# A decoder layer's opening on one core: first norm from token rows, transfers issued on arrival of others, and the third weight unit in the output buffer

## The chip, the cores and the metric

The kernel runs on one core of one Trainium2 chip. The metric is the device time in microseconds (us) of one execution; the time before is the median of three runs. Engines are named as in the profile: PE is TensorE's matmul (PEld its weight load), DVE is VectorE, ACT is ScalarE, POOL is GpSimd, SP is SyncE, which here only issues transfers.

## What is computed

One layer of a decoder over 256 tokens of width 1024, in float32. Only its opening matters here:

```python
def rms_norm(x, g):
    xf = x.astype(jnp.float32)
    y = xf * lax.rsqrt(jnp.mean(xf * xf, axis=-1, keepdims=True) + RMS_EPS)
    return (y * g.astype(jnp.float32)).astype(x.dtype)

def swiglu(h, w_gate, w_up, w_down):
    return (jax.nn.silu(h @ w_gate) * (h @ w_up)) @ w_down

x = x + 0.5 * swiglu(rms_norm(x, norm_ffn1[l]), ffn1_gate[l], ffn1_up[l], ffn1_down[l])
```

After it come a mixing sub-layer (projections, attention, a recurrent part), a second SwiGLU of the same form (hidden width 2816 in both) and a last norm.

## The kernel before, in words

**Layout.** The residual `x` lies with its features on the partitions, as 8 tiles of 128 features by 256 tokens. Weights come in units of 1024 by 256 (1 MB): unit 0 is the first 256 gate columns, unit 1 the first 256 up columns, unit 2 the next gate columns, and so on; even units use slot 0 and odd ones slot 1 of `raw`, `whi` and `wlo`. Each float32 operand is split into a high and a low part: ACT copies `raw` into `whi` (`hi`, L521, or in quarters `first_hi`, L531), DVE subtracts (`lo`, L875, or `first_lo`, L885), and PE multiplies three pairs (hi by lo, lo by hi, hi by hi). A unit on PE is a chunk of 48 matmuls of 128x128 by 128x256.

**The norm's factor is applied late.** PE multiplies with `x` times the gain only. The factor 1/rms of each token, `rstd` (128 partitions by 256 tokens, the same in every partition), is multiplied in when DVE takes the product out of PSUM: L923 takes the gate product (`gate_taken`) and L942 the up product (`up_taken`). PE's chunk of unit 2 writes the bank that L923 empties, so `chunk(1, 0)` waits for `lo_ready` 3 and for `gate_taken` 1; `chunk(1, 1)`, unit 3, waits for `lo_ready` 4 and `up_taken` 1.

**SP's queue** issues, in this order and with no wait among them: the first constants (128 columns of identity, 128 of 1/1024, two of epsilon), `x` by tokens in two halves of its columns (`x_in0`, `x_in1`), unit 0 in two halves (`w0_in`, then `w_landed[0]`), unit 1, the other constants (848 KB), twelve small rows of vectors, and `rel_bias`. Every later unit n waits for `lo_ready` n-1, which frees its slot: unit 2 for the end of unit 0's low parts, unit 3 for unit 1's.

**PE** runs six warm-up products of the identity with itself as soon as the first constants are there, transposes the gain rows (L1513) and then `x` in four pairs of tiles (L1518) into banks 2, 3, 6 and 7, runs three more warm-up products, and starts `first_chunk(0)`, which goes on pair by pair as `hlo_f` and `w_lo` come. In `first_chunk(1)`, before its third pair, stands `mean_square(0)`: a product of 1/1024 with the summed squares, which gives every partition the mean square of each token. Then come a transpose of the vector rows (L1474) and the bias row's product (L1477), and then chunks without end.

**ACT** loads its table early, then alternates `h_hi` (the gained `x`, high part, L551) and `first_hi` of unit 0. It then squares the four pairs out of PSUM into `x_sq`, which lies in the output buffer (L621), makes the four quarters of unit 1's high part, and takes the root (`rms_root`, L537), for which another table is loaded; the first Silu (L566) has a third. **DVE** alternates `gained_lo` (L894) and `first_lo`, copies `x` from PSUM to SBUF (L1013) after the squares, makes unit 1's low parts, takes the reciprocal of 128x256 (L912) and enters `ffn`. **POOL** adds the four tiles of squares up (L420, L424, L417), clears two pads (L429, L430), and later sends the bias rows and loads the small "lora" matrices, the first of which waits for the bias row's copy (`bias_row_sb`, L967 to L432).

Of the kernel before, what the change touches and what calls it, by code (L numbers as in the profile page):

```python
# [123 lines left out]
first_hi first_lo sq_first sq_one sq_sum last_sq mean_sq rms_ready rstd_ready gained hhi_ready hlo_ready  # L124
# [20 lines left out]
def trunk(nc, A, consts, out):  # L145
    bias_dram = nc.dram_tensor("bias_rows", (H, 16, 384), F32, kind="Internal").ap()
    with ExitStack() as ctx:
# [20 lines left out]
        idle = sb("idle", [P, 2])  # L168

# [22 lines left out]
        with ExitStack() as sc:  # L192
# [10 lines left out]
            x_sq = out_tok[:].rearrange("p a d -> p (a d)").rearrange("p (q m t) -> p q m t", q=4, m=2)  # L203
# [121 lines left out]
        def _(sp):  # L325
# [12 lines left out]
            for f, base, down in FFN:  # L338
                if f == 0:
                    sp.dma_start(raw[0][:, 0:4], gate_w[0][:, 0:4, 0:W]).then_inc(sg["w0_in"], 16)  # L340
                    sp.dma_start(raw[0][:, 4:KD], gate_w[0][:, 4:KD, 0:W]).then_inc(w_landed[0], 16)
                else:
                    load(base, base // 2, 0, gate_w[f][:, :, 0:W])
                load(base + 1, base // 2, 1, up_w[f][:, :, 0:W])
                if f == 0:
# [53 lines left out]
        def _(pool):  # L399
            def squares(q, signal, first, step, pairs=4):  # L400

                for c in range(pairs):
                    pool.wait_ge(signal, first + c * step)
                    pair = x[:, 2 * c:2 * c + 2]
                    if c == 0:
                        pool.wait_ge(sg["mean_sq"], q)
                        nc.gpsimd.tensor_tensor(sqsum[:], pair, pair, ALU.mult).then_inc(sg["sq_sum"], 1)  # L407
                    else:
                        pool.wait_ge(sg["sq_sum"], 5 * q - 1 + c)
# [3 lines left out]
                halves_sum(5 * q - 1 + pairs)  # L413
# [5 lines left out]
            pool.wait_ge(sg["sq_first"], 2)  # L419
            nc.gpsimd.tensor_tensor(sqsum[:], x_sq[:, 0], x_sq[:, 1], ALU.add).then_inc(sg["sq_sum"], 1)  # L420
            for q in range(2, 4):
                pool.wait_ge(sg["sq_first"], q + 1)
                pool.wait_ge(sg["sq_sum"], q - 1)
                nc.gpsimd.tensor_tensor(sqsum[:], sqsum[:], x_sq[:, q], ALU.add).then_inc(sg["sq_sum"], 1)  # L424
# [90 lines left out]
        def _(act):  # L515
# [10 lines left out]
            def first_hi(n, i):  # L526

                if i % 2 == 0:
                    act.wait_ge(sg["w0_in"] if n + i == 0 else w_landed[n], 16)
# [4 lines left out]
            def rms_root(q, cols=slice(0, T)):  # L534

                act.wait_ge(sg["mean_sq"], q + 1)
# [22 lines left out]
            def ffn(f, base, down):  # L559
# [28 lines left out]
                body(0, nexts(0))  # L588
# [24 lines left out]
            act.wait_ge(sg["x_ffn_even"], 1)  # L613
            nc.scalar.activation(idle[:, 0:1], idle[:, 0:1], ACT.Identity)
# [1411 lines left out]
```

## Time and profile before

| what | before |
|---|---|
| median of 3 runs | 653.97 us (652.64 to 654.25) |
| the profiled execution, its own time | 653.73 us |
| its span | 651.9 us |
| PE busy, DVE busy, ACT busy, POOL busy | 635.1, 424.9, 295.8, 95.9 us |
| mean granted TensorE clock | 0.996 |

The span is what the trace covers; 1.83 us of the profiled execution's own time lie around it. A row of the trace names line, engine, operation, output from input. A matmul's row shows its whole passage through the array, which overlaps the next one, so matmuls of 0.28 us follow each other in less than that.

### The profile page before, as it was taken

The numbers are of one execution on the slowest core, as the hardware profiler recorded it, in microseconds if no ns is written. First come the engines' busy times: TensorE is split into PE (matmuls) and PEld (weight loads), VectorE is DVE, ScalarE is ACT, GpSimd is POOL, SyncE is SP. The second block draws the span as 40 slices with busy tenths as digits, with TensorE's granted clock in tenths as the row PEclk, the third lists the DMA queues.
The fourth block names the chain that finished last, engine by engine and source line by source line (L and its number), as shares of the span: only waits on it lengthen the run. The fifth ranks groups of instructions, "written<-read, shape, count | busy, mean of one in ns | idle before, by whom it ended". The sixth has DMA issues, their size and how long they took to land.

```text
span 651.9 us, 15471 instructions
## 1 busy us (share of the span) xinstructions
PE 635.1 (97%) x6726; PEld 620.3 (95%) x6726; DVE 424.9 (65%) x487; ACT 295.8 (45%) x337; POOL 95.9 (15%) x95
## 2 busy tenths in 40 slices
PE   7899999999999999999998999999999999999996
PEld 7799999999999999999987889999999999999996
DVE  4866787665556369968993337877766666665662
ACT  5544454443334174425654544545533444443331
POOL 0325800000112100020004423006000000000120
PEclk9999999999999999999999999999999999999998
DMA  7686555655555335593242222356555566546541
GB/s 258 196 254 208 174 167 185 190 177 178 178 177 193 102 130 182 185 201 113 98 131 67 68 95 73 125 169 193 174 166 180 188 193 192 174 154 197 167 148 64
DMA packets 100607, 105.37 MB, mean 162 GB/s; under 512 B 2196, under 2 KB 98684, under 8 KB 100564
## 3 DMA queue, kind: packets, MB, share of 16 engines
q1 hardware_dynamic: 99348, 101.45, 49.3%
q0 software_dynamic: 1056, 3.02, 2.1%
q8 instruction: 34, 0.56, 0.4%
q10 hardware_dynamic: 160, 0.27, 0.1%
q14 instruction: 9, 0.07, 0.0%
HBM read 103.48 MB, written 1.25 MB: 161 GB/s over the span
## 4 chain that ended last, share of the span: by engine, by line
PE 90%; DVE 5%; ACT 1%; DMA 1%; issue 1%; SPq 0%; DVEq 0%; ACTq 0%
PE two L1404 26%; PE two L1406 25%; PE two L1405 25%; PE two L1400 11%; DVE w_lo L875 2%; DMA w_raw<-in_ffn_gate 1%; DVE hlo_f L894 1%; PE two L1660 1%; PE two L1662 1%; PE two L1661 1%; DVE w_lo L885 0%; PE two L1803 0%; DVE x L1013 0%; ACT KK L763 0%; DVE rstd L912 0%
## 5 line engine op out<-in xcount | busy, mean ns | idle before, releaser
L521 ACT ACTIVATE w_hi<-w_raw 128x2048 fp32r<-128x2048 f32 (+1 forms) x88 | 166.0, 1887 | 264.7 <-PE two L1406 233.8
L875 DVE TENSOR_TENSOR w_lo<-w_raw,w_hi 128x2048 fp32r<-128x2048 f32 (+1 forms) x88 | 203.9, 2317 | 88.5 <-ACT w_hi L521 88.1
L1404 PE MATMUL two<-hlo_f,w_hi 128*128 128x256 f32 x656 | 185.9, 283 | 2.2 <-DVE w_lo L875 2.2
L1406 PE MATMUL two<-hhi_f,w_hi 128*128 128x256 f32 x656 | 184.9, 282 | 0.0
L1405 PE MATMUL two<-hhi_f,w_lo 128*128 128x256 f32 x656 | 184.8, 282 | 0.0
L1404 PEld LDWEIGHTS two<-hlo_f,w_hi 128*128 128x128 f32 x656 | 123.0, 188 | 3.3 <-DVE w_lo L875 3.3
L1405 PEld LDWEIGHTS two<-hhi_f,w_lo 128*128 128x128 f32 x656 | 124.0, 189 | 0.0
L1406 PEld LDWEIGHTS two<-hhi_f,w_hi 128*128 128x128 f32 x656 | 123.9, 189 | 0.0
L1404 PE MATMUL two<-hid_lo_t,w_hi 128*128 128x256 f32 x352 | 99.9, 284 | 0.0
L1406 PE MATMUL two<-hid_hi_t,w_hi 128*128 128x256 f32 x352 | 99.3, 282 | 0.0
L1405 PE MATMUL two<-hid_hi_t,w_lo 128*128 128x256 f32 x352 | 99.3, 282 | 0.0
L1404 PE MATMUL two<-hlo_m,w_hi 128*128 128x256 f32 x288 | 83.7, 290 | 0.3 <-DVE w_lo L875 0.3
L1405 PE MATMUL two<-hhi_m,w_lo 128*128 128x256 f32 x288 | 80.5, 279 | 0.0
L1406 PE MATMUL two<-hhi_m,w_hi 128*128 128x256 f32 x288 | 80.4, 279 | 0.0
L1405 PEld LDWEIGHTS two<-hid_hi_t,w_lo 128*128 128x128 f32 x352 | 66.5, 189 | 0.0
L1404 PEld LDWEIGHTS two<-hid_lo_t,w_hi 128*128 128x128 f32 x352 | 66.2, 188 | 0.2
L1406 PEld LDWEIGHTS two<-hid_hi_t,w_hi 128*128 128x128 f32 x352 | 66.4, 189 | 0.0
L1404 PEld LDWEIGHTS two<-hlo_m,w_hi 128*128 128x128 f32 x288 | 54.2, 188 | 3.8 <-issue 2.3
L1406 PEld LDWEIGHTS two<-hhi_m,w_hi 128*128 128x128 f32 x288 | 54.3, 188 | 0.1
L1405 PEld LDWEIGHTS two<-hhi_m,w_lo 128*128 128x128 f32 x288 | 54.3, 189 | 0.0
L407 POOL TENSOR_TENSOR sqsum<-x 128x512 f32<-128x512 f32 x3 | 3.1, 1040 | 249.1 <-DVE x L991 220.5
L942 DVE TENSOR_TENSOR prod<-two,rstd 128x512 f32<-128x512 f32 x22 | 15.2, 692 | 26.0 <-PE two L1406 26.0
(327 smaller groups left out, 966.2 us busy)
## 6 DMA issues: line engine op xcount, KB each, us to landing
w_raw<-in_ffn_up SPq DMA_DIRECT2D x22, 1024.0 KB, 5.4
w_raw<-in_ffn_gate SPq DMA_DIRECT2D x21, 1024.0 KB, 5.3
w_raw<-in_w_in SPq DMA_DIRECT2D x20, 1024.0 KB, 5.1
w_raw<-in_ffn_down SPq DMA_DIRECT2D x16, 896.0 KB, 4.8
w_raw<-in_ffn_down SPq DMA_DIRECT2D x8, 1024.0 KB, 5.2
w_raw<-in_w_out SPq DMA_DIRECT2D x4, 1024.0 KB, 5.9
w_raw<-in_proj_a SPq DMA_DIRECT2D x4, 512.0 KB, 3.5
w_raw<-in_proj_b SPq DMA_DIRECT2D x4, 512.0 KB, 4.4
```

The source lines that it names most:

```text
L407: nc.gpsimd.tensor_tensor(sqsum[:], pair, pair, ALU.mult).then_inc(sg["sq_sum"], 1)
L521: nc.scalar.activation(whi[slot][:, 0:kts], raw[slot][:, 0:kts], ACT.Copy).then_inc(sg["hi_ready"], 1)
L875: nc.vector.tensor_tensor(wlo[slot][:, 0:kts], raw[slot][:, 0:kts], whi[slot][:, 0:kts].bitcast(F32), ALU.subtract).then_inc(sg["lo_ready" ...
L894: last = nc.vector.scalar_tensor_tensor(out=hl[:, 2 * j + m], in0=src, scalar=v(GAINS[q], 2 * j + m), in1=hh[:, 2 * j + m].bitcast(F32), o ...
L942: nc.vector.tensor_tensor(prod[:], bank[1][:].rearrange("p (m t) -> p m t", m=2), rstd2, ALU.mult).then_inc(sg["up_taken"], 1)
L1400: return mm(dst, lhsT, rhs, start=start, stop=True, skip_group_check=True)
L1404: mm(dst, whi[slot][:, k_, cols], xl, start=start, stop=False)
L1405: mm(dst, wlo[slot][:, k_, cols], xh, start=False, stop=False)
L1406: return mm(dst, whi[slot][:, k_, cols], xh, start=False, stop=stop)
L1660: mm(dst, hlo_m[:, k_, ts], whi[c % 2][:, k_], start=k_ == 0, stop=False)
L1661: mm(dst, hhi_m[:, k_, ts], wlo[c % 2][:, k_], start=False, stop=False)
L1662: last = mm(dst, hhi_m[:, k_, ts], whi[c % 2][:, k_], start=False, stop=k_ == KD - 1)
```

## The change

SP: the second half of unit 0 is issued when the first half of `x` has landed, unit 1 when the second half has, and unit 2 when the first half of unit 0 has landed. Unit 2 goes into the output buffer (`raw2`), so it needs no free slot. The other constants, the vector rows and `rel_bias` follow, and then unit 3, which waits for `lo_ready` 2 as before.

The first norm: ACT squares `x_tok` (tokens on the partitions, 128 by 512, four times) with an accumulated sum per token, DVE adds the two halves' sums, ACT takes the root of a 128x2 tile, DVE its reciprocal, and DVE multiplies the identity by each token's factor and by 1024 (two tiles of 128x128). PE multiplies 1/1024 with these, which puts every token's factor into all partitions, before the fourth pair of `first_chunk(1)`. ACT copies the result to `rstd`. POOL takes no part; its adds are gone. Unit 2's high and low parts are made in halves of 128x1024 straight after the root and after the two diagonal tiles. The table of the root is the one loaded at the start, and a Silu of one column loads the Silu table after the copy.

Order: unit 1's quarters come before the squares, each followed by one square on ACT and by one copy of `x` on DVE. The transpose of the vector rows and the bias row's product go behind unit 2's chunk on PE, and DVE's `bias_sb` goes behind body 1. POOL's clearing of pads waits for the first chunk. PE's warm-up products use a tile of ones that DVE writes, so they wait for no transfer: seven, the transpose of the gains, three, the transposes of `x`, four.

```diff
@@ SP
-                    sp.dma_start(raw[0][:, 0:4], gate_w[0][:, 0:4, 0:W]).then_inc(sg["w0_in"], 16)
-                    sp.dma_start(raw[0][:, 4:KD], gate_w[0][:, 4:KD, 0:W]).then_inc(w_landed[0], 16)
...
+                    sp.dma_start(raw[0][:, 0:4], gate_w[0][:, 0:4, 0:W]).then_inc(w_landed[0], 16)
+                    sp.wait_ge(sg["x_in0"], 16)
+                    sp.dma_start(raw[0][:, 4:KD], gate_w[0][:, 4:KD, 0:W]).then_inc(sg["w0_in"], 16)
+                    sp.wait_ge(sg["x_in1"], 16)
+                    load(1, None, 1, up_w[0][:, :, 0:W])
+
+                    sp.wait_ge(w_landed[0], 16)
+                    sp.dma_start(raw2, gate_w[0][:, :, W:2 * W]).then_inc(w_landed[0], 16)
                     sp.dma_start(cst[:, C_FIRST:C_ALL], consts[:, C_FIRST:C_ALL]).then_inc(sg["const_in"], 16)
                     for name in list(VECS)[1:]:
                         vector_rows(sp, name, sg["vec_in"])
                     sp.dma_start(rel[:], A["rel_bias"]).then_inc(sg["vec_in"], 16)
+                    load(3, None, 1, up_w[0][:, :, W:2 * W])
...
-                with sp.Fori(1, NG) as i:
+                with sp.Fori(1 if f else 2, NG) as i:
@@ POOL
-            pool.wait_ge(sg["sq_first"], 2)
-            nc.gpsimd.tensor_tensor(sqsum[:], x_sq[:, 0], x_sq[:, 1], ALU.add).then_inc(sg["sq_sum"], 1)
...
-            halves_sum(3)
-
...
-            pool.wait_ge(sg["sq_sum"], 4)
+            pool.wait_ge(sg["multiplied"], 1)
@@ ACT
-                body(0, nexts(0))
+                body(0, nexts(0) if f else [lambda: None, nexts(0)[1]])
...
-            nc.scalar.activation(idle[:, 0:1], idle[:, 0:1], ACT.Identity)
+            act.wait_ge(sg["x_ffn_odd"], 1)
+            nc.scalar.activation(idle[:, 0:1], idle[:, 0:1], ACT.Sqrt)
             act.wait_ge(sg["gain1_ready"], 1)
             for j in range(4):
                 h_hi(0, j, hhi_f)
                 first_hi(0, j)
             for j in range(4):
-                act.wait_ge(sg["hlo_ready"], j + 1)
-                nc.scalar.activation(x_sq[:, j], bank[X_BANKS[j]][:].rearrange("p (c t) -> p c t", c=2),
-                                     ACT.Square).then_inc(sg["sq_first"], 1)
-            for j in range(4):
                 first_hi(1, j)
-            rms_root(0)
+                act.wait_ge(sg[f"x_in{j // 2}"], 16)
+                nc.scalar.activation(h_f[:, 2 * j:2 * j + 2].rearrange("p m t -> p (m t)"),
+                                     x_tok[:, j % 2, j // 2 * (D // 2):(j // 2 + 1) * (D // 2)], ACT.Square,
+                                     accum_out=tok[:, j:j + 1]).then_inc(sg["first_norm"], 1)
+            act.wait_ge(sg["first_norm"], 5)
+            nc.scalar.activation(tok[:, 6:8], tok[:, 4:6], ACT.Sqrt, bias=cst[:, C_EPS:C_EPS + 1],
+                                 scale=1.0 / D).then_inc(sg["rms_ready"], 1)
+
+            act.wait_ge(w_landed[0], 32)
+            act.wait_ge(sg["multiplied"], 1)
+            nc.scalar.activation(whi[0][:, 0:4], raw2[:, 0:4], ACT.Copy).then_inc(sg["first_hi"], 1)
+            nc.scalar.activation(whi[0][:, 4:KD], raw2[:, 4:KD], ACT.Copy).then_inc(sg["hi_ready"], 1)
+            act.wait_ge(sg["first_norm"], 8)
+            nc.scalar.activation(rstd[:, 0:T], bank[4][:, 0:T], ACT.Copy).then_inc(sg["first_norm"], 1)
+            nc.scalar.activation(idle[:, 0:1], idle[:, 0:1], ACT.Silu)
             ffn(0, N_FFN1, N_DOWN1)
@@ DVE
             for j in range(4):
-                dve.wait_ge(sg["sq_first"], j + 1)
+                first_lo(1, j)
                 nc.vector.tensor_copy(x[:, 2 * j:2 * j + 2], bank[X_BANKS[j]][:].rearrange("p (c t) -> p c t", c=2))\
                     .then_inc(sg["x_loaded"], 1)
-            for j in range(4):
-                first_lo(1, j)
-            inverse_rms(0)
+            dve.wait_ge(sg["first_norm"], 4)
+            nc.vector.tensor_tensor(tok[:, 4:6], tok[:, 0:2], tok[:, 2:4], ALU.add).then_inc(sg["first_norm"], 1)
+            dve.wait_ge(sg["rms_ready"], 1)
+            nc.vector.reciprocal(tok[:, 6:8], tok[:, 6:8]).then_inc(sg["rstd_ready"], 1)
+            dve.wait_ge(sg["rstd_ready"], 1)
+            for j in range(2):
+                nc.vector.tensor_scalar(prod[:, 0, j * P:(j + 1) * P], ident, tok[:, 6 + j:7 + j], float(D),
+                                        ALU.mult, ALU.mult).then_inc(sg["first_norm"], 1)
+            dve.wait_ge(sg["first_hi"], 7)
+            nc.vector.tensor_tensor(wlo[0][:, 0:4], raw2[:, 0:4], whi[0][:, 0:4].bitcast(F32), ALU.subtract)\
+                .then_inc(sg["first_lo"], 1)
+            dve.wait_ge(sg["hi_ready"], 3)
+            nc.vector.tensor_tensor(wlo[0][:, 4:KD], raw2[:, 4:KD], whi[0][:, 4:KD].bitcast(F32), ALU.subtract)\
+                .then_inc(sg["lo_ready"], 1)
+            dve.wait_ge(sg["first_norm"], 9)
@@ PE
-                    if n == 1 and pair == 2:
-                        mean_square(0)
+                    if n == 1 and pair == 3:
+                        pe.wait_ge(sg["first_norm"], 7)
+                        for j in range(2):
+                            last = part(bank[4][:, j * P:(j + 1) * P], mat("mean_d"), prod[:, 0, j * P:(j + 1) * P], j == 0)
+                        last.then_inc(sg["first_norm"], 1)
...
                     first_chunk(1)
+                    chunk(1, 0)
...
                         .then_inc(sg["bias_row"], 1)
+                    chunk(1, 1)
...
+            pe.wait_ge(sg["x_ffn_even"], 1)
+            warm(7)
             pe.wait_ge(sg["first_in"], 16)
-            for i in range(6):
-                part(bank[4][:, 0:P], ident, ident, True)
             pe.wait_ge(sg["gain1_in"], 16)
             nc.tensor.transpose(bank[5][:, 0:KD], vec_rows[0:KD], ident[0:KD, 0:KD]).then_inc(sg["gain1_T"], 1)
+            warm(3)
...
-            for i in range(3):
-                part(bank[4][:, 0:P], ident, ident, True)
+            warm(4)
```

## Rows read from the trace of the kernel before

**Rows 1.** The page: busy time by engine, and the chain's shares by engine.

```profile
PE 635.1 (97%) x6726; PEld 620.3 (95%) x6726; DVE 424.9 (65%) x487; ACT 295.8 (45%) x337; POOL 95.9 (15%) x95
...
PE 90%; DVE 5%; ACT 1%; DMA 1%; issue 1%; SPq 0%; DVEq 0%; ACTq 0%
```

**Rows 2.** The chain that ended last, opening: start, length in us, what.

```profile
2.17 7.20 DMA w_raw<-in_ffn_gate
...
14.43 0.60 DVE w_lo L885
15.03 2.40 DVE x L1013 x4
17.43 0.78 DVE w_lo L885
...
22.68 1.76 DVE rstd L912
24.47 0.69 DVE silu L923
25.16 2.21 DVE w_lo L875
```

**Rows 3.** Timeline of PE: start, us, row, idle before it and what ended it.

```profile
18.34 0.36 PE L1400 MATMUL two<-hlo_f,w_hi 128*128 128x256 f32 x1 [1.39 <-DVE w_lo L885]
...
24.85 0.25 PE L1474 MATMUL two<-cst,vec_rows 96*128 96x96 f32 x1
25.03 0.81 PE L1477 MATMUL two<-cst,rel 32*8 32x384 f32 x2
27.41 0.39 PE L1404 MATMUL two<-hlo_f,w_hi 128*128 128x256 f32 x1 [1.57 <-DVE w_lo L875]
```

**Rows 4.** Stretch table, all engines: stretch, its length, busy time and count by engine.

```profile
27.40:33.40 6.00, 5.99 (x50) 5.99 (x51) 4.60 (x5) 2.09 (x3) 0.80 (x1) 1.00 0.74 203
```

**Rows 5.** Waits of PE from 34 to 640 us: total, times, longest.

```profile
PE two L1404 <- DVE w_lo L875: 1.3, 3, 0.6
```

**Rows 6.** Timeline of DVE, unit 1's low parts.

```profile
17.34 4.29 DVE L885 TENSOR_TENSOR w_lo<-w_raw,w_hi 128x512 fp32r<-128x512 f32 x4
```

**Rows 7.** Groups by form over the whole span: busy us, mean ns.

```profile
L728 ACT ACTIVATE w_hi<-w_raw 128x1024 fp32r<-128x1024 f32 x8 | 8.2, 1051 | 0.0
...
L537 ACT ACTIVATE rstd<-two,cst 128x2 f32<-128x2 f32 x1 | 0.3, 262 | 1.8 <-PE two L1400 1.8
...
L632 ACT ACTIVATION_READ_ACCUMULATOR lg<-lg,stat 128x1 f32 x16 | 3.0, 186 | 0.0
...
L1348 DVE TENSOR_TENSOR w_lo<-w_raw,w_hi 128x1024 fp32r<-128x1024 f32 x4 | 4.9, 1224 | 0.0
...
L1096 DVE TENSOR_SCALAR lg<-lg,stat 128x128 f32<-128x128 f32 x8 | 2.3, 282 | 0.0
...
L1088 DVE TENSOR_SCALAR stat<-stat 128x2 f32<-128x2 f32 x8 | 1.4, 169 | 0.3
```

**Rows 8.** Timeline of ACT, opening.

```profile
15.53 2.25 ACT L531 ACTIVATE w_hi<-w_raw 128x512 fp32r<-128x512 f32 x4
...
24.47 1.28 ACT L566 ACT_TABLE_LOAD   x1
```

**Rows 9.** Timeline of SP's queue, opening.

```profile
3.81 4.10 SPq L346 DMA_DIRECT2D cst<-in_consts  x1
...
12.22 0.32 SPq L349 DMA_DIRECT2D rel<-in_rel_bias  x1
```

**Rows 10.** Issue to landing: both `x` halves; then units 0 (halves) and 1.

```profile
DMA to landing us min/median/max: 3.6/4.9/6.2
...
DMA to landing us min/median/max: 7.2/8.2/10.6
```

**Rows 11.** Issue to landing of the seven whole units issued between 20 and 60 us.

```profile
DMA to landing us min/median/max: 5.3/5.4/5.9
```

**Rows 12.** Stretch table as in rows 4; the last two columns are DMA share and GB/s.

```profile
0.00:5.00 5.00, 2.03 (x9) 2.03 (x10) 0.09 (x2) 1.49 (x2) 0.20 (x4) 1.00 0.58 183
5.00:10.00 5.00, 5.00 (x28) 4.36 (x26) 1.04 (x3) 1.45 (x4) 0.00 (x0) 1.00 1.05 357
```

More of the change, by code:

```diff
@@ L168, in trunk @@
         idle = sb("idle", [P, 2])
+        tok = sb("tok", [P, 8])
         def mat(name):
@@ L349, in _ @@
                     sp.dma_start(rel[:], A["rel_bias"]).then_inc(sg["vec_in"], 16)
-                with sp.Fori(1, NG) as i:
+                    load(3, None, 1, up_w[0][:, :, W:2 * W])
+                else:
+                    load(base, base // 2, 0, gate_w[f][:, :, 0:W])
+                    load(base + 1, base // 2, 1, up_w[f][:, :, 0:W])
+                with sp.Fori(1 if f else 2, NG) as i:
                     load(2 * i + base, None, 0, gate_w[f][:, :, bass.ts(i, W)])
@@ L528, in first_hi @@
                 if i % 2 == 0:
-                    act.wait_ge(sg["w0_in"] if n + i == 0 else w_landed[n], 16)
+                    act.wait_ge(sg["w0_in"] if n == 0 and i == 2 else w_landed[n], 16)
                 ks_ = slice(2 * i, 2 * i + 2)
@@ L962, in nexts @@
                     return [lambda s=s: lo(2 * i + (base + 2 + s), s) for s in range(2)]
-                body(0, nexts(0))
-                if f == 0:
-                    dve.wait_ge(sg["bias_row"], 1)
-                    nc.vector.tensor_tensor(bias_sb[:], bank[6][0:H, 0:384], cst[0:H, C_NEG:C_NEG + 384],
-                                            ALU.add).then_inc(sg["bias_row_sb"], 1)
+                body(0, nexts(0) if f else [lambda: None, nexts(0)[1]])
                 if f == 0:
@@ L971, in ffn @@
                         body(i, nexts(i))
+                        if i == 1:
+                            dve.wait_ge(sg["bias_row"], 1)
+                            nc.vector.tensor_tensor(bias_sb[:], bank[6][0:H, 0:384], cst[0:H, C_NEG:C_NEG + 384],
+                                                    ALU.add).then_inc(sg["bias_row_sb"], 1)
                 with dve.Fori(1 if f else 9, NG - 1) as i:
@@ L999, in ffn @@
                         gained_lo(1, j)
-            nc.vector.memset(idle[:, 0:1], 0.0).then_inc(sg["x_ffn_even"], 1)
-            nc.vector.memset(idle[:, 1:2], 0.0).then_inc(sg["x_ffn_odd"], 1)
+            nc.vector.memset(silu[:, 0, 0:P], 1.0).then_inc(sg["x_ffn_even"], 1)
+            nc.vector.memset(idle[:], 0.0).then_inc(sg["x_ffn_odd"], 1)
             dve.wait_ge(sg["gain1_T"], 1)
@@ L1484, in ffn @@
                     chunk(0, 1)
-                with pe.Fori(1, NG) as i:
+                with pe.Fori(1 if f else 2, NG) as i:
                     chunk(i, 0)
@@ L1506, in ffn, with warm @@
                         last.then_inc(sg["multiplied"], 1)
+            def warm(count):
+                for i in range(count):
+                    part(bank[4][:, 0:P], silu[:, 0, 0:P], silu[:, 0, 0:P], True)
+            pe.wait_ge(sg["x_ffn_even"], 1)
+            warm(7)
             pe.wait_ge(sg["first_in"], 16)
-            for i in range(6):
-                part(bank[4][:, 0:P], ident, ident, True)
             pe.wait_ge(sg["gain1_in"], 16)
             nc.tensor.transpose(bank[5][:, 0:KD], vec_rows[0:KD], ident[0:KD, 0:KD]).then_inc(sg["gain1_T"], 1)
+            warm(3)
             for q in range(4):
```

26 lines of the change are left out of this document (9 added, 17 removed).

## The prediction

> **What bounds the kernel now.** I read the page first: PE is busy 97% of the span and carries 90% of the chain that ended last [rows 1]. Everything behind the opening is PE at full pace: a stretch of 6.00 us holds 50 matmuls [rows 4], so one takes 0.12 us and a chunk of 48 takes 5.76 us, and from 34 to 640 us PE waits for low parts 1.3 us in all [rows 5]. The change can therefore earn only what PE loses before it runs without gaps, and each microsecond by which that point moves is one off the end.
>
> Next the chain in order of time [rows 2]. To 15.03 us it is DVE, fed by the first half of unit 0 landing at 2.17 + 7.20 = 9.37 us; then four copies of x, unit 1's low parts, the reciprocal, the gate product, unit 2's low part. PE's timeline shows what that costs [rows 3]: first_chunk(0) is over at 18.34 - 1.39 = 16.95 us, PE is idle 1.39 us, first_chunk(1) lasts to 24.85 us with small gaps, and after the two small products PE is idle 1.57 us to 27.41. Unit 2's chunk starts there, so unit 3's starts at 27.41 + 5.76 = 33.17 us. That is the point I move.
>
> **The change, part by part.** *What starts everything.* DVE is free of its first phase at 15.03 us [rows 2]. The waits of DVE in that phase hang on unit 0's first half, whose place in SP's queue is unchanged. Whether holding later transfers back makes it land sooner no row shows. Two bounds. Nothing: it stays at 9.37. Most: 183 GB/s over 5 us and 357 GB/s behind that [rows 12] are about 0.92 MB by 5 us and 1.95 MB by 7.9 us, when x's second half has landed (issue near 1.7 plus 6.2 [rows 10]); 1.18 MB would have been enough for it, so 0.77 MB of later transfers, 2.1 us, went first. Unit 0's first half has 1.70 MB up to its end, reached at 7.2 us; x's first half landed near 1.2 + 3.6 = 4.8 us [rows 10], 0.5 us after the 0.66 MB up to its end had moved at these rates; with so short a lag unit 0's half would land at 7.7, 1.7 us sooner (estimates from the rows named). I take nothing, because the landings from x's second half to unit 1 all come about 2 us behind their bytes, as they would if some of the 16 engines were simply behind on all they hold: holding back what is queued behind does not speed those up. The 1.7 us stay in the range. The Trainium skill speaks against this part too (DMA: Bandwidth & Descriptors, section "Queues, rings and completion order"): each engine consumes the descriptors of its ring in order. By that rule a transfer behind gives way already, and the gain is zero; by the byte count above the sum would end 1.7 us earlier.
>
> *Unit 1 before the squares.* Unit 1 lands at 3.23 + 10.6 = 13.8 us before [rows 10]. Now it is issued at about 7.95; a unit alone takes 5.4 us [rows 11], which is 13.35, and with unit 0's second half still ahead of it I keep 13.8. Its first quarter's high part takes 2.25/4 = 0.56 us [rows 8], so it is ready at 14.4, before DVE is free; it may be 0.6 us late at no cost. DVE then alternates: 4 x (0.60 + 0.60) = 4.80 us, to 19.83 [rows 2]. The low parts took 4.29 us for four [rows 6], against 2.4 at 0.60 each, while POOL was adding; POOL is idle now, so I take 0.60. ACT does 0.56, as much for a square of the same size, and up to 0.19 for reading the accumulator [rows 7, 8]: 4 x 1.3 = 5.2 us, to 19.0, hidden behind DVE. PE gets a quarter every 1.2 us and needs 1.44 for it, so the idle 1.39 us [rows 3] go and first_chunk(1) runs from 16.95 to 22.7 and, with the spread product (at most 0.5 us, since all that first_chunk(1) holds beyond its 48 matmuls now, gaps too, is 24.85 - 18.34 - 5.76 = 0.75 [rows 3]), to 23.2.
>
> *The norm.* From 19.83: add 0.17, root 0.26, with hand-offs about 0.05: 20.3 [rows 7]. On DVE reciprocal 0.17 and two diagonal tiles of 0.28: 21.1. PE reaches the fourth pair at 16.95 + 3 x 1.44 = 21.3, so it hardly waits. Gone are POOL's adds, the 128x256 reciprocal of 1.76 us [rows 2] and one table load of 1.28 us from the path.
>
> *Unit 2.* It lies in the output buffer by about 16 us (issued near 9.5 behind unit 1) and is wanted at 20.3. ACT: half a unit is 1.05 us, ready at 21.35 and 22.35. DVE: 1.22 us per half [rows 7], from 21.35 to 22.57, then to 23.7 (rows of one engine overlap by 0.08). Only then comes the gate product, 0.69 us [rows 2]: 24.4. Unit 2's chunk waits for it, since it writes that bank. This is the new last wait: PE is done at 23.2 and idles 1.2 us. The copy to rstd (about 22.3 to 22.8) and the Silu table (1.28 us, to 24.1 [rows 8]) lie beside it.
>
> *The two small products* stood in PE's gap; now they stand on its path: from 24.85 to 25.84 us they are busy [rows 3], less about 0.3 by which a matmul's passage overlaps the next, 0.7 us. bias_sb on DVE and POOL's bias and lora transfers move back by some 9 us; these cost nothing as long as the lora halves, whose last issue waits for chunk 6 either way, keep their place.
>
> *The start on PE.* Earlier warm-up moves the transposes by a few tenths, but unit 0's landing at 9.37 sets what follows: nothing.
>
> **Sum.** Unit 2's chunk starts at 24.4, ends at 30.15, small products 30.85: unit 3's chunk starts there instead of at 33.17, 2.3 us sooner. Unit 3 must then be ready: issued when unit 1's low parts are done (15.03 + 3 x 1.2 + 0.6 = 19.2), landed at 24.6 [rows 11], its high part (after the first silu, 25.1; two halves of 1.05 [rows 7] make 2.0) and its low part of 2.2 us [rows 2]: 29.3, 1.5 us of room. Against the profiled execution's 653.73 this is 651.4; that execution lies 0.24 below the median 653.97.
>
> **Rivals.** *A: transfers do come sooner.* Unit 0's half at 7.7 and unit 1 by 12.6 shift the whole DVE chain by 1.7 us: 649.7. For it: the 0.77 MB above. Against: the constant lag. Half of it, 650.5, is as good. *B: unit 1 is late,* because three waits stand between issues where none did, or because unit 2 and the constants share the engines with it. Unit 1 and 2 together are 2.1 MB from 9.0 us at 357 GB/s [rows 12]: if they ended together, unit 1 would land at 15 and DVE start at 15.6, 0.6 us later: 652.0; with the constants mixed in too, 17.3 us and 653.0 or more. Against: units issued before it had landed in order. *C: the squares need another table than the root.* Then two loads of 1.28 us enter ACT's chain, the squares end at 20.3, the root at 21.8, 1.5 us later: 652.9. For it: before, the squares ran on a table that the root had to replace. Against: Copy and Identity run on every table there, and Square may. *D, slower: unit 3 behind SP's queue.* The constants took SP 4.10 us to issue and it was done with the small rows at 12.54 us [rows 9], 8.7 us in all; from 9.9 that is 18.6. If it is t instead, unit 3's chunk starts at t + 5.4 + 2.0 + 2.2: it costs from t = 21.2 on, turns slower than before at t = 23.6, and 653.7 + (t - 23.6) is the time: 656.7 at t = 26.6, were the constants to hold SP 12 us with two whole units outstanding. Against: half the backlog of before stands ahead of them.
>
> **How the numbers follow.** A measurement of this kernel can tell about 0.3%, 2 us, from no change: faster means below 652.0. Base case 0.46 (651.4, own spread 0.5 us for the small hand-offs, of which a sixth lies above 652.0), A 0.26, B 0.13, C 0.07, D 0.04, the rest (0.04) beyond A or mixed. Faster: 0.38 + 0.26 + 0.03 from B + 0.02 = 0.69. Slower: 0.03. Same: 0.28. The range goes from A's end less 0.2 to C's, which takes in most of B: 649.5 to 652.9.
>
> **What would show it.** Right: unit 0's half lands at 9.4; DVE rows of 0.6 us alternate with copies to 19.8; PE has no gap between the first two chunks; one gap of 1.2 us before L1404 ended by DVE's gate product; unit 3's chunk near 30.8. Wrong: a landing before 8.5 (A), ACT waiting for unit 1 past 14.5 (B), a table load before the first square (C), ACT waiting for unit 3 past 26.7 (D), or PE losing more than before later on, where I expect nothing to move.

## The result, and the profile after

The changed kernel took 645.97 us (median of 4 runs, 644.80 to 647.58) against 653.67 us for the kernel before on the same chip (652.64 to 654.25): ratio 0.9886, 95% interval 0.9859 to 0.9913. Forecast were 651.4 us and a range of 649.5 to 652.9. The sign was right; the gain is 7.7 us where 2.3 were forecast, and the time lies outside the range.

The page of the kernel after: busy time by engine, and the chain's shares by engine, as in [rows 1].

```profile
PE 630.7 (98%) x6738; PEld 615.9 (96%) x6738; DVE 423.1 (66%) x491; ACT 295.5 (46%) x343; POOL 90.6 (14%) x91
...
PE 88%; DVE 5%; DMA 3%; ACT 2%; issue 0%; SPq 0%; DVEq 0%; ACTq 0%
```

PE has 12 more instructions and is busy 4.4 us less. Nothing that the prediction names makes the same matmuls shorter. To see where the time went I set the starts of the same work side by side (ACT's copies of whole units; most start when PE frees a slot, the one at 424 us when its transfer has landed, in both kernels):

| stretch | before, us | after, us | gain so far | gain in the stretch |
|---|---|---|---|---|
| opening, to ACT's copy of a unit near 45 us | 45.05 | 42.12 | 2.93 | 2.9 |
| to 68 us | 68.09 | 66.10 | 1.99 | -0.9 |
| rest of the first FFN, to 159 us | 158.81 | 155.81 | 3.00 | +1.0 |
| to 328 us | 328.01 | 324.78 | 3.23 | +0.2 |
| small matmuls of the mixing, to 424 us | 423.89 | 417.12 | 6.77 | +3.5 |
| second FFN, to 617 us | 616.59 | 607.97 | 8.62 | +1.9 |
| span | 651.9 | 643.0 | 8.9 | +0.3 |

So only a third of this pair's gain is made in the opening. (The profiled executions lie 653.73 - 644.80 = 8.9 us apart, more than the medians.) Four things have to be explained: the opening, a loss near 60 us, a small steady gain in both FFNs, and a jump in the mixing.

**The opening** is what the prediction drew. The chain that ended last, of the kernel after, in order of time (start, us, what):

```profile
1.66 4.95 DMA x_tok<-in_x
6.63 6.99 DMA w_raw<-in_ffn_up
13.64 0.64 ACT w_hi L531
14.30 0.69 DVE w_lo L895
14.99 0.60 DVE x L1023
...
18.59 0.60 DVE x L1023
...
22.94 0.61 DVE silu L933
23.55 0.14 issue
23.68 0.36 PE two L1426
```

VectorE alternates low parts and copies at 0.60 us each. PE waits 0.95 us inside the first chunk (to 9.59 us), 0.58 us for the diagonal tiles (to 20.46 us), and last and longest for the gate product, as its timeline shows; the two small products stand behind unit 2's chunk:

```profile
23.68 0.36 PE L1426 MATMUL two<-hlo_f,w_hi 128*128 128x256 f32 x1 [1.12 <-DVE silu L933]
...
29.46 0.25 PE L1500 MATMUL two<-cst,vec_rows 96*128 96x96 f32 x1
29.63 0.81 PE L1503 MATMUL two<-cst,rel 32*8 32x384 f32 x2
```

Forecast were 24.4 for the chunk and a gap of 1.2. What the prediction has otherwise is the first line of the chain: unit 1 is now on it, by way of the wait for `x`.

**The loss near 60 us.** Waits of the kernel after from 44 to 66 us (us in total, times, longest):

```profile
ACT w_hi L521 <- DMA w_raw<-in_ffn_gate: 5.4, 1, 5.4
...
PE two L1426 <- DVE w_lo L885: 0.9, 1, 0.9
```

and who shared the engines with that unit, in the timelines of POOL and SP of the same kernel:

```profile
42.04 0.80 POOL L432 DMA_DIRECT2D bias_rows<-bias_sb  x1 [25.39 <-DVE bias_sb L980]
42.83 0.94 POOL L435 DMA_DIRECT2D x_tok<-in_w_lora_a  x1
43.74 0.91 POOL L437 DMA_DIRECT2D x_tok<-in_a_lora_a  x1
44.62 0.78 POOL L441 DMA_DIRECT2D out_tok<-in_g_lora_a  x1
...
46.54 0.37 SPq L331 DMA_DIRECT2D w_raw<-in_ffn_gate  x1
```

POOL waited 25.39 us for the bias row that the change had put behind unit 2's chunk, and then issued four transfers in three microseconds that used to be spread from 32.54 to 45.25 us. The weight unit issued behind them at 46.54 took 9.1 us to land, where [rows 11] have 5.3 to 5.9.

**The jump in the mixing.** By PE's own rows the kernel after is 3.3 us ahead at 338 us of the kernel before, about 5.9 us at 384 and at 415 us, and about 7 us at 443 us. Waits of PE from 338 to 430 us, first the kernel before:

```profile
PE two L1400 <- issue: 2.7, 4, 1.1
```

and after:

```profile
PE two L1422 <- issue: 0.6, 1, 0.6
```

"issue" is time in which the engine waited for nothing that the profile shows. Four such stalls, between 343 and 384 us, have become one: 2.1 of the 2.6 us gained there. What the last 1 us, behind 415 us, is made of is not shown.

**The steady gain.** ACT's copies of whole units from 90 to 140 us, count, durations, first and last start; before:

```profile
L521 ACT ACTIVATE w_hi<-w_raw x9: 1916/1917/1917, 91.1 to 137.2; 128x2048 fp32r<-128x2048 f32 x9
```

and after:

```profile
L521 ACT ACTIVATE w_hi<-w_raw x9: 1916/1917/1920, 88.9 to 134.4; 128x2048 fp32r<-128x2048 f32 x9
```

Eight chunks take 46.1 us before and 45.6 after: 5.76 and 5.70 us each, 0.1200 and 0.1187 us for the same matmul at the same granted clock of 1.00. The change adds one tile of 8 floats a partition (`tok`), which moves every tile allocated behind it by 32 bytes. PE's moving operands (`hhi_f`, `hlo_f`, the hidden tiles) are among them; the weights (`w_hi`, `w_lo`) lie ahead of it and stay.

### The profile page after: what moved, and what is told of

Read it like the earlier page. It is cut to its first block, busy times and chain, and to the rows that moved or that the text cites. A ratio compares the mean times of both kernels' runs of the same rounds, so it can differ in the third digit from the quotient of the medians.

```text
span 643.0 us, 15489 instructions
## 1 busy us (share of the span) xinstructions
PE 630.7 (98%) x6738; PEld 615.9 (96%) x6738; DVE 423.1 (66%) x491; ACT 295.5 (46%) x343; POOL 90.6 (14%) x91
## 4 chain that ended last, share of the span: by engine, by line
PE 88%; DVE 5%; DMA 3%; ACT 2%; issue 0%; SPq 0%; DVEq 0%; ACTq 0%
PE two L1426 26%; PE two L1428 24%; PE two L1427 24%; PE two L1422 10%; DVE w_lo L885 2%; DMA w_raw<-in_ffn_gate 1%; ACT w_hi L521 1%; DMA w_raw<-in_ffn_up 1%; DMA x_tok<-in_x 1%; PE two L1691 1%; DVE hlo_f L904 1%; PE two L1693 1%; PE two L1692 1%; PE two L1834 0%; DVE w_lo L895 0%
## 5 line engine op out<-in xcount | busy, mean ns | idle before, releaser
L521 ACT ACTIVATE w_hi<-w_raw 128x2048 fp32r<-128x2048 f32 (+1 forms) x87 | 164.2, 1887 | 257.7 <-PE two L1428 231.7
```

The costliest lines, as they stand in the source:

```text
L521: nc.scalar.activation(whi[slot][:, 0:kts], raw[slot][:, 0:kts], ACT.Copy).then_inc(sg["hi_ready"], 1)
```

## The experiments

The kernel before took 652.84 to 653.98 us (median) beside each of these. "Place" is the offset, modulo 1024 bytes in a partition, at which the compiled kernel puts PE's moving operand: in the FFNs 736 before and 768 after, in the mixing 928 and 960.

### The kernel after once more

> The changed kernel once more, beside the others, as their yardstick. What is to be explained: 645 to 647 us against 653 to 654, where the opening alone gives 2.9 us (unit 3's chunk at 30.3 instead of 33.2). Between the two traces a matmul of the feed-forward stages takes 0.1187 instead of 0.1200 us (about 3 us over both stages), and stalls of 0.6 to 1.3 us that the old trace had at four places between 343 and 384 us are absent (about 3 us). Theory S (it lies in the program): this run shows 0.1187 us again and 643 to 646 us. Rival V (it lies in the execution, a luckier one): the matmul's pace or the stalls differ from those of the first profile.

647.36 us (645.39 to 647.99), ratio 0.9901 (0.9886 to 0.9917): somewhat less gain than in the first comparison. Its profile (span 646.0 us) shows one way in which executions of this kernel differ. PE's timeline near 60 us, and the stretch table with the granted clock in the third column from the right:

```profile
60.92 0.41 PE L1426 MATMUL two<-hlo_f,w_hi 128*128 128x256 f32 x1 [2.05 <-DVE w_lo L885]
```

```profile
56.00:62.00 6.00, 3.95 (x31) 3.75 (x30) 3.41 (x3) 4.34 (x3) 6.00 (x10) 0.93 0.16 53
62.00:66.00 4.00, 4.00 (x26) 4.00 (x26) 3.15 (x3) 0.63 (x1) 4.00 (x4) 0.68 0.91 274
```

and the second of these stretches in the first profile of the same kernel:

```profile
62.00:66.00 4.00, 4.00 (x36) 4.00 (x35) 2.15 (x2) 0.00 (x0) 4.00 (x6) 1.00 0.96 302
```

Here PE waited 2.05 us for the late unit instead of 0.9, and then the granted clock went to its lower level (1.2 GHz) from about 61.2 to 64.6 us, where matmuls follow each other every 0.213 us. Ten matmuls fewer fit into the second stretch. By the starts of ACT's copies (45.05 and 68.09 us before, 42.12 and 66.10 us in the first profile, 41.88 and 68.50 us in this one) the late unit costs 0.9 us in one execution and 3.6 in the other. This doesn't explain the higher median: the other five executions have mean clocks of 0.997 to 0.999, where this one has 0.994, and took 645.4 to 648.0 us.

### The place alone: e1 and its reverse, e2

e1 is the kernel before with the new tile allocated and never used:

```diff
+        tok = sb("tok", [P, 8])
```

> The kernel before, with only the change's new tile of 8 floats allocated where the change allocates it and used by nobody: every tile behind it moves by 32 bytes in SBUF. Theory S-place: the matmul's pace follows from where its operands lie, so this shows 0.1187 us per matmul in the feed-forward stages and gains 2 to 3 us (about 651). Rival: the pace is the execution's or the code's, and this kernel equals the kernel before, 0.1200 us and 653.7.

650.08 us, ratio 0.9948 (0.9934 to 0.9961). Eight chunks take 45.6 us, as after:

```profile
L522 ACT ACTIVATE w_hi<-w_raw x9: 1912/1917/1922, 90.8 to 136.4; 128x2048 fp32r<-128x2048 f32 x9
```

An unused tile makes the kernel before 3.4 us faster, and it does so although this profile loses about 1.4 us in the opening: unit 2's chunk starts at 26.28 us, behind a wait of PE of 1.58 us, and half a microsecond later the granted clock is at its lower level.

```profile
26.80:30.20 3.40, 3.40 (x18) 3.40 (x18) 3.00 (x4) 1.73 (x3) 0.00 (x0) 0.50 0.77 225
```

e2 is the kernel after with that tile laid over the first floats of `sq`, so that nothing moves:

```diff
-        tok = sb("tok", [P, 8])
+        tok = sq[:, 0, 0:8]
```

> The changed kernel, with its 8 floats laid in a tile that is free in the opening, so that nothing moves in SBUF. Theory S-place: 0.1200 us per matmul again, 2 to 3 us slower than the changed kernel (about 648.5). Rival: as the changed kernel, 646.

650.32 us, ratio 0.9959 (0.9944 to 0.9974), slower than the kernel after by 3.0 us between the medians and 3.8 us between the ratios, and its chunks are back at 5.76:

```profile
L521 ACT ACTIVATE w_hi<-w_raw x9: 1917/1918/1918, 89.4 to 135.5; 128x2048 fp32r<-128x2048 f32 x9
```

Both directions agree: 3 to 4 us of the gain are where tiles lie. That it is the moving operand, and not another of the tiles that moved with it, was not separated.

### The position of PE's code: e3

The kernel before, with the chunks of units 2 and 3 written out ahead of the loop, as the change has them:

```diff
-                with pe.Fori(1, NG) as i:
+                if f == 0:
+                    chunk(1, 0)
+                    chunk(1, 1)
+                with pe.Fori(1 if f else 2, NG) as i:
```

> The kernel before, with units 2 and 3 on PE written out instead of run by the loop, as the change does: same work in the same order, 96 matmuls more of PE's code ahead of all that follows. Theory C (the stalls between 343 and 384 us hang on where PE's code lies as it is fetched): they move or go, up to 3 us faster (about 651), at an unchanged pace of 0.1200 us. Rival: no difference, 653.7, and the stalls stay.

649.73 us, ratio 0.9956 (0.9938 to 0.9973): 2.9 us faster by the ratio, 3.7 between the medians, with chunks at 5.76. Waits of PE from 338 to 430 us:

```profile
PE two L1400 <- issue: 0.8, 2, 0.5
```

By PE's rows the profile gains 2.5 us on the kernel before between 338 and 384 us and 2.9 us to 446 us, where e1, which has the tile and not the code, keeps 2.5 us of stalls. (The other 1.1 us by which this profile is shorter lie in the opening: unit 0 landed sooner.) So the stalls go with the position of the code that follows.

That they are instruction fetch is argued, not shown, since the profile gives these stalls no releaser. The DMA view speaks for it. It has a queue of instruction packets of 16 KB; in the kernel before, from 338 to 392 us:

```profile
q8 instruction: 12, 0.20, 1.6%
```

By their times in the trace, one ends at 343.34, 352.59, 367.64 and 381.83 us, and the four stalls begin at 343.62, 353.24, 368.67 and 382.86 us, 0.3 to 1.0 us behind them. In e3 and in the kernel after the three stalls that are left begin 0.7 to 1.0 us behind such a packet. But no stall follows the other eight of the twelve, and why these four do is open. The Trainium skill (Runtime: NRT & Kernel Launch, section "Instruction fetch mechanics") says that fetch is mostly hidden in straight code and stalls behind a taken branch whose target lies outside the window of code at hand. PE's code has no loop in this stretch, so if the stalls are fetch, straight code didn't hide it here.

### Holding transfers back: e4, and later e12

e4 is the kernel after without SP's two waits for `x`:

```diff
-                    sp.wait_ge(sg["x_in0"], 16)
...
-                    sp.wait_ge(sg["x_in1"], 16)
```

> The changed kernel without SP's two waits on the halves of x: unit 0's second half and unit 1 are issued at once, as before. In five profiles unit 0's first half has now landed anywhere from 8.1 to 9.4 us, with the waits and without. Theory N (holding back does nothing that lasts): the opening and the total are as in the changed kernel, 645 to 647.5, and unit 1 lands no later. Rival H (holding back gives x and unit 0 the engines): x's second half lands about 1 us later than the 6.6 us of the changed kernel, unit 0's first half about 9.4, and unit 2's chunk starts 1 us later; 647 to 648.5.

646.18 us, ratio 0.9890 (0.9875 to 0.9905). Unit 0's first half is copied at 7.91 us without the waits (8.08 and 8.88 us in e11 and e12, below) and at 7.9 to 9.3 with them (8.09 in the first profile): holding back does not bring it sooner. It was 9.39 in the profile of before, but 8.31 in both e1 and e3, which issue as before does: the landing of that one execution was late.

What the waits do is delay unit 1. e12 makes the same edit to a kernel without the other disturbances (e8, below), on one chip with it:

> The same kernel as e8_best, for comparison on one chip with the next three. Both theories: 640.3 us within 1; FFN chunks at 5.60 us, no wait on the late unit near 60 us.

> e8_best without SP's waits for the two halves of x, so that unit 0's second half and unit 1 are issued as early as in the kernel before. Theory H (holding back costs): unit 1 is there when ScalarE is done with unit 0, so the wait of 1.2 to 2.1 us goes, VectorE alternates from about 14.0 instead of 14.6 to 15.2, the root runs at 18.5 instead of 19.6, unit 2's chunk starts near 22.8 instead of 24.0: about 1 us faster than e8_again, 639.3 us. Rival (the earlier issues slow x and unit 0, so the opening is as long): unit 0's first quarter is copied later than 8.3 us and unit 2's chunk stays at 23.5 to 24; no difference.

e8 641.20 us (ratio 0.9808, 0.9791 to 0.9825), e12 639.50 (0.9785, 0.9770 to 0.9800). The intervals overlap, so the times don't decide, though the medians differ by 1.7 us. The profiles show what the waits do. ACT's timeline in e8:

```profile
8.33 0.63 ACT L532 ACTIVATE w_hi<-w_raw 128x512 fp32r<-128x512 f32 x1 [1.03 <-DMA w_raw<-in_ffn_gate]
...
14.67 0.63 ACT L532 ACTIVATE w_hi<-w_raw 128x512 fp32r<-128x512 f32 x1 [1.97 <-DMA w_raw<-in_ffn_up]
```

and in e12:

```profile
8.88 0.63 ACT L530 ACTIVATE w_hi<-w_raw 128x512 fp32r<-128x512 f32 x1 [1.84 <-DMA w_raw<-in_ffn_gate]
...
13.45 0.63 ACT L530 ACTIVATE w_hi<-w_raw 128x512 fp32r<-128x512 f32 x1 [0.19 <-DMA w_raw<-in_ffn_up]
```

Unit 0 is 0.55 us later here, no more than executions of one kernel differ by, and unit 1 is 1.2 us sooner; unit 2's chunk starts at 23.81 instead of 24.71. That is 1 us later than the 22.8 expected, and both signs of the rival are there (unit 0 later than 8.3, the chunk between 23.5 and 24). One profile can't tell an unlucky landing from a cost of the earlier issues; e4 and e11, with unit 0 at 7.91 and 8.08 us, speak for the landing. Over all profiles two sums hold to 0.1 us: without a late unit 1 the chunk starts 14.9 us behind ACT's first copy of unit 0 (e2, e4, e6, e12: 14.92, 14.92, 14.93, 14.93; forecast were 24.4 - 9.37 = 15.0), and with it 10.04 us behind the first copy of unit 1 (after, e5, e7, e8, e9). The first copy of unit 1 waits 0.2 to 2.3 us for its transfer in ten of eleven profiles with the two waits; in the one other, e6, unit 0 was late itself. By the two sums, and if unit 0 lands as it does with them, the waits cost 0 to 1.8 us of the opening (an estimate).

### The order of POOL's transfers: e5

```diff
-            pool.wait_ge(sg["bias_row_sb"], 1)
-            pool.dma_start(bias_dram, bias_sb[:].unsqueeze(1).to_broadcast([H, 16, 384])).then_inc(sg["bias_out"], 16)
...
+            pool.wait_ge(sg["bias_row_sb"], 1)
+            pool.dma_start(bias_dram, bias_sb[:].unsqueeze(1).to_broadcast([H, 16, 384])).then_inc(sg["bias_out"], 16)
```

> The changed kernel with POOL's transfer of the bias rows moved behind its four loads of the lora matrices, so that those again go out one per chunk instead of four in a row at 42 to 48 us, and POOL no longer waits for the bias row ahead of them. In the three profiles of the changed opening so far a weight unit issued at 46.5 took 9.1 us to land and the gain over the kernel before shrank by 1.0 to 3.4 us between 45 and 68 us. Theory B (four loads in a row delay that unit): the loss goes, 1 to 3 us faster than the changed kernel, 643 to 646. Rival: the unit is late for another reason (the reads of POOL's own queue, an instruction fetch) and nothing changes.

645.55 us, ratio 0.9880 (0.9864 to 0.9896). POOL's timeline has its loads spread again:

```profile
30.68 1.09 POOL L432 DMA_DIRECT2D x_tok<-in_w_lora_a  x1 [14.17 <-PE two L1428]
37.38 0.90 POOL L434 DMA_DIRECT2D x_tok<-in_a_lora_a  x1 [5.62 <-PE two L1428]
43.07 0.76 POOL L438 DMA_DIRECT2D out_tok<-in_g_lora_a  x1 [4.79 <-PE two L1428]
```

and PE waits for no low part from 50 to 80 us. The cause is shown: the wait for the bias row, with four loads queued behind it. The profile is only 0.2 us shorter than that of the kernel after because its opening was 0.75 us longer (unit 2's chunk at 24.43, unit 1 being later). Against the second run of the kernel after it gains 1.8 us, the intervals overlapping.

### How far the place goes: e6 and e7

The kernel after with a wider tile, 48 floats (e6) or 16 (e7) instead of 8.

> The changed kernel with its small tile made 192 bytes instead of 32: the feed-forward operands lie 160 bytes further than in the changed kernel, at 928 modulo 1024 and at 32 modulo 64, the mixing stage's at 96 modulo 1024. So far: feed-forward at 736 (32 modulo 64) 0.1200 us, at 768 (0 modulo 64) 0.1187; mixing at 928 0.1167, at 960 0.1178. Theory M (a matmul's pace follows the place modulo 1024 of its moving operand): feed-forward at 928 runs at 0.1167, some 6 us faster, about 640. Rival A (only the alignment to 64 bytes counts in the feed-forward stages): 0.1200 again, 4 us slower, about 650.

> The changed kernel with its small tile made 64 bytes: feed-forward operands at 800 modulo 1024 and 32 modulo 64, mixing at 992. Rival A: 0.1200 us in the feed-forward stages, about 650. Theory M: a pace of its own, between 0.1165 and 0.1190, since it lies between 768 (0.1187) and 928 (0.1167).

In e6 the pace came as theory M had it and the time did not: 645.50 us (ratio 0.9884, 0.9866 to 0.9901) where about 640 were expected. Eight chunks take 44.8 us, 5.60 each. Beside the first profile of the kernel after it gains 4.7 us in the two FFNs, and loses 2.5 us near 60 us (a wait of 2.05 us and the lower clock level), 1.7 us in the mixing, whose operands moved too, and 0.3 us in the opening.

```profile
L521 ACT ACTIVATE w_hi<-w_raw x9: 1917/1917/1920, 91.3 to 136.1; 128x2048 fp32r<-128x2048 f32 x9
```

e7 (one run, 649.18 us) has 5.64 in the first FFN and 5.70 in the second, at one and the same place. Pace by place over all profiles, us per matmul:

| place | profiles | pace |
|---|---|---|
| 736 | before, e2, e3 | 0.1200 in all |
| 768 | after (2), e1, e4, e5, e9 | 0.1187 in all |
| 800 | e7 | 0.1173, then 0.1187 |
| 928 | e6, e8 (2), e8b, e10, e11, e12 | 0.1167, in three of seven profiles with stretches at 0.1178 |

In the mixing the change's 32 bytes made chunks slower, so far as they can be read: 5.60 us at 928, 5.65 at 960, 5.68 at 96, 5.76 at 992. The two places with the slowest pace, 736 and 992, lie 256 bytes apart; whether the pace repeats with that step was not tried. So the place decides among paces, and something else that differs between executions of one kernel, and within one, has a part in it. What it is stays open.

### The output buffer: e9

Unit 2 goes into `raw[0]` again, as soon as unit 0's low parts are made.

```diff
-                    sp.wait_ge(w_landed[0], 16)
-                    sp.dma_start(raw2, gate_w[0][:, :, W:2 * W]).then_inc(w_landed[0], 16)
+                    load(2, None, 0, gate_w[0][:, :, W:2 * W])
```

> The kernel after, with unit 2 loaded into the first raw buffer as soon as unit 0's low parts have been made from it (as in the kernel before) in place of the output buffer. Theory N: the output buffer buys nothing, since VectorE reaches unit 2's low parts only at about 19.5 us after the root and the release at about 12.2 plus 6 to 7 us of landing ends at 18.5 to 19.2: 0 to 0.5 us slower than the kernel after at the same time, unit 2's chunk within 0.5 us of 23.7. Rival (the output buffer carries part of the gain of the opening): unit 2's low parts wait for the transfer, unit 2's chunk comes 1 to 2 us later, at 24.7 to 25.7, and the time is 1 to 2 us longer.

647.19 us, ratio 0.9912 (0.9889 to 0.9935), against 645.97 and 647.36 for the kernel after. Unit 2's chunk starts at 24.62, 0.9 us later than expected, but 10.04 us behind the first copy of unit 1, exactly as with the output buffer: unit 1 was late again. Unit 2 was issued at 13.82 us, landed at 19.4 and was wanted at 20.44, so the buffer bought nothing here. In an opening with unit 1 in time it may: e4 wanted unit 2 at 18.65 us, with unit 0 copied 0.25 us sooner, which would leave unit 2 some 0.5 us late (an estimate from the two profiles; not run).

### Putting it together: e8, and e8b

e8 is e5 with the new tile over `sq`, and 192 unused bytes ahead of the FFN's operands alone. e8b is e5 with the wide tile of e6.

```diff
-        tok = sb("tok", [P, 8])
+        tok = sq[:, 0, 0:8]
...
+            pad = sb("pad", [P, 48], scope=sc)
```

> POOL's bias rows behind its four lora loads, the new small tile laid over the first floats of sq (it takes no space of its own), and 192 bytes of unused space ahead of the FFN's operands alone, so that their bf16 operand of 4 x 4 x 512 starts at 928 modulo 1024 and the mixing's stays at 928. Theory P (a matmul's pace follows the place of its moving operand): 5.60 us for 48 matmuls in the FFN's first part as in e6_pad192 against 5.695 in the kernel after, and 5.60 in the mixing as in the kernel before against 5.653; from e5's 645.5 us that is 20 chunks of the first part x 0.095 = 1.9, the second part about as much again, and 10 units of the mixing x 0.05 = 0.5: about 641 us (639 to 643). Rival (the place isn't all, as two paces at 800 suggest): the FFN's pace comes out at 5.69 or more, and the time stays at 645 to 646. Both: no wait of PE on the late unit near 60 us, and the granted clock stays at 1.00 there.

> POOL's bias rows behind its four lora loads, and the new small tile 192 bytes wide, which moves both operands: the FFN's to 928 modulo 1024, the mixing's to 96. Theory P: 5.60 us for 48 matmuls in the FFN's first part, 5.68 in the mixing, no wait at 60 us: about 1.5 us below e6_pad192 for the wait that goes, so 643 to 644 us, and 0.8 us above e8_best (10 units x 0.08 in the mixing). Rival: the time is that of e6_pad192 within 0.5 us, the wait at 60 us being made up later.

640.32 us (ratio 0.9804, 0.9781 to 0.9826) and 640.85 us (0.9809, 0.9785 to 0.9832). e8's time came out as expected, its pace in the first FFN did not: 0.1178 us where 0.1167 were expected. e8b is 2 to 3 us faster than expected: I had priced the late unit at 1.5 us and left the lower clock level behind it out. Most of its first FFN ran at 0.1178 too; when e8 was run again, all of it ran at 0.1167.

### VectorE's order and the last wait: e10 and e11

e10 is e8 with VectorE's order turned back:

```diff
             for j in range(4):
-                first_lo(1, j)
                 nc.vector.tensor_copy(x[:, 2 * j:2 * j + 2], ...)
+            for j in range(4):
+                first_lo(1, j)
```

> e8_best with VectorE's order of the opening turned back alone: the four copies of x first, then unit 1's four low parts. By the prediction's chain the order as such costs nothing, since the last wait before unit 2's chunk is the gate product: the root ends when copies and low parts are done, in either order. And where unit 1 is late, the copies fill the wait: VectorE ends both at the last quarter's high part plus 0.7, root near 18.9 instead of 19.6, unit 2's chunk 0.5 to 0.8 us sooner than in e8_again, measured from the first high part of unit 1. Rival (the order carries the gain): the first chunk of unit 1 on PE starts 1.2 us or more later and ends behind the gate product, unit 2's chunk 0.5 to 1.5 us later.

640.29 us (0.9794, 0.9779 to 0.9809), 0.9 below e8, within both intervals. PE starts unit 1 later,

```profile
17.03 0.36 PE L1424 MATMUL two<-hlo_f,w_hi 128*128 128x256 f32 x1 [1.32 <-DVE w_lo L896]
```

but unit 2's chunk starts at 23.48, 9.27 us behind the first copy of unit 1 instead of 10.04. With unit 1 late the new order costs 0.8 us on this path. With unit 1 in time it was not compared.

e11 puts a reciprocal of 128x256, whose result nobody uses, ahead of the gate product. It was made from e12, without the two waits, and not from e8 as its expectation says; so it is read against e12's 639.50.

```diff
             dve.wait_ge(sg["first_norm"], 9)
+            nc.vector.reciprocal(sqsum[:, 0], rstd[:, 0:T])
```

> e8_best with one more reciprocal of 128x256 on VectorE, ahead of the gate product; its output isn't used. If the gate product is the last wait before unit 2's chunk, the 1.76 us that the old norm's reciprocal took are paid in full: PE's gap before L1427 goes from 1.1 to 2.9 us, the later unit 3 takes it up in part or not at all, and the time is 1.7 us above e8_again. Rival (PE's chunks or the late unit 3 bind): less than 0.8 us.

642.51 us (0.9838, 0.9812 to 0.9864), 3.0 above e12. PE's timeline and a stretch:

```profile
24.61 0.47 PE L1426 MATMUL two<-hlo_f,w_hi 128*128 128x256 f32 x1 [2.75 <-DVE silu L932]
```

```profile
24.00:28.00 4.00, 3.39 (x16) 3.42 (x17) 2.79 (x4) 2.95 (x3) 0.00 (x0) 0.59 0.74 247
```

The gap grows from 1.14 to 2.75 us, and behind it the granted clock falls to its lower level, 0.59 of full speed as the mean of this stretch. Time ahead of the gate product is paid in full, 1.6 us, and in this execution again by the clock, 1.6 us. The 3.0 us between the medians are not simply their sum: this profile also has its second FFN at 0.1178 us, and an execution of e11 with a mean clock of 0.999 took 641.93 us, 2.4 above e12's median.

## Why the prediction was wrong

**What held.** *The opening's chain.* Alternating rows of 0.60 us, the root, the diagonal tiles, unit 2's low parts and the gate product as the last wait came as worked out, to 0.1 us from the landing of unit 0. Unit 1 landed at 13.6, forecast 13.8. PE's gap was 1.12 against 1.2, the small products took about 0.9 us against 0.7 (29.46 to 30.37); e11 shows that the gate product does decide. There is luck in it. Unit 1 was issued at 6.63 us and not at 7.95, and took 7.0 us to land and not 5.4 to 5.9; the two misses cancel. And in the pair of profiles the opening gained 2.9 us where 2.3 were forecast, but 1.1 of them are the late landing of unit 0 in the profile of before: against e3, where unit 0 was copied at 8.31, unit 3's chunk starts 1.8 us sooner (30.37 against 32.19). *Rival C* did not come: no table load stands ahead of the squares. *Rival D* did not come: SP was free for unit 3 at 15.3, since the constants took it 2.06 us and not 4.10.

**What was taken from one execution.** "What starts everything" set unit 0's first half at 9.37 us and argued that it would stay. It was 8.1, and not by the change, although the prediction had named a landing before 8.5 as the sign of rival A. That gave the opening no more, because unit 1 was next: *rival B* in small. The step "it may be 0.6 us late at no cost" was right for a DVE free at 15.03; with DVE free at 13.7 us unit 1, landed at 13.6 and copied by 14.3, was 0.6 us late. *Rival A* fell: unit 0's first half comes no sooner with less behind it (e4). By the rule of the Trainium skill that the prediction weighed (DMA: Bandwidth & Descriptors, section "Queues, rings and completion order") the gain is zero, and the traces agree (copied at 7.91 to 8.88 us without the waits, at 7.9 to 9.3 with them). The waits have a price, though: unit 1 is issued only when `x` has landed, and in ten of eleven profiles ACT then waits for it.

**The step that failed** is the first one: "the change can therefore earn only what PE loses before it runs without gaps", with "losing more than before later on, where I expect nothing to move". It took 5.76 us for a chunk, and the gaps among the mixing's matmuls, for properties of the work. Both changed with things that the diff does and that I costed at nothing without naming them: a tile of 32 bytes ahead of the other tiles (e1: 3.4 us), and PE's code for two chunks more ahead of the mixing (e3: 2.9 us). More than twice as much time lies there as in all the steps that I worked out. Why the pace goes with the place, and why some stalls went, stays open.

**A second step failed** with the other sign: "bias_sb on DVE and POOL's bias and lora transfers move back by some 9 us; these cost nothing". I asked whether the last lora load keeps its place (it does: 48.02 us, 51.01 before) and not what the first three, let go at once behind the bias rows, do to the unit beside them: 0.9 us in one execution, 3.6 in another.

With the terms as measured: 1.8 to 2.9 (opening) + 3.4 (place) + 2.9 (code) less 0.9 to 3.6 (late unit) is 4.5 to 8.3 us; the runs gave 7.7 and 6.1.

The kernel that comes out of this, e12, takes 639.50 us, ratio 0.9785: it keeps the norm from token rows, drops the two waits, puts POOL's bias transfer last and moves the FFN's operands to 928 modulo 1024. e10's order was not tried on it.

## What to carry to other kernels

When PE is the bound, a change that adds a tile or a few instructions can move more time by where everything behind it comes to lie than by what it does. Take the same matmul's pace in both traces before crediting the change, and test the place with an unused tile. A wait in a queue must be priced with all that is queued behind it, and with what those transfers will share the engines with when they are let go together. And read a landing time from several executions before building on a microsecond of it.

## What the runs showed of the hardware that I had not expected

A matmul of 128x128 by 128x256 with the same operands and a granted clock of 1.00 takes 0.1200, 0.1187, 0.1178, 0.1173 or 0.1167 us, going with the place of the tiles (32 bytes are enough) and with something else that differs between executions.

PE stood still four times for 0.46 to 1.12 us among small matmuls for no reason that the profile names, each time 0.3 to 1.0 us behind a packet of 16 KB of instructions, and with 96 more matmuls of code ahead of them two or one such stalls were left, 0.8 us (e3) and 0.6 us (after) in all.

The lower clock level came within 1.3 us of the end of a wait of PE of 2.05 us in the kernel after (second run) and in e6, of 2.22 us in e7, of 2.75 us in e11, and of only 1.58 us in e1. It did not come behind waits of 1.57 and 1.58 us at the same place in before and e3, nor behind waits of 0.9 to 1.6 us near 60 us (after in its first run, e2, e4, e9). So the length of the wait alone does not decide. It cost about 1.5 us on top of the wait: 1.4 us by ACT's copies of e1 beside e3, 1.6 us by those of e11 beside e12.
